# A fused two-block transformer kernel: the front rebuilt around channel-major inputs, and the retention stage reordered

## The reference, cut to what matters

```python
# layer 0 of the first block
mem_n = rmsnorm(mem, g_mem)
h = rmsnorm(x, g_mix[0])
mem_k, mem_v = split(mem_n @ w_mem_kv[0])
p = h @ w_in_a[0]
u, q_mem = p[..., :1536], p[..., 1536:]
a, gate = split(u + b_glu)
v = causal_dwconv(a * sigmoid(gate), w_dw_a, b_dw_a)   # 31 taps, 768 channels
mix = silu(layernorm(v, ln_g, ln_b))
mem_o = memory_attention(q_mem, mem_k, mem_v)          # 4 heads of 64
x = x + concat([mix, mem_o]) @ w_out[0]
x = x + conv_ffn(rmsnorm(x, g_ffn[0]), ...)
# layer 1: forgetting attention, memory attention, conv_ffn, final rmsnorm
# second block, layer 0: retention, 4 heads
s = (q @ k.T) * decay;  o = s @ v                      # in chunks of 128 tokens
o = (o - mu) * rsqrt(var + EPS) * gn_gain
h = h + (silu(gate) * o) @ w_out
# then a per-layer embedding, sparse attention, a second embedding, rmsnorm
```

## Time and profile before

| | |
|---|---|
| median of 3 runs | 1319.33 us (1319.16 to 1319.84) |
| profiled execution, its own time | 1318.41 us |
| its span in the trace | 1316.6 us |
| PE busy in the span | 1246.5 us (95%) |
| DVE, ACT busy | 893.2 us (68%), 641.8 us (49%) |
| granted TensorE clock, mean | 0.977 |
| DMA | 198.44 MB, mean 151 GB/s |

### The profile page before, as it was taken

The page is one execution under the profiler, slowest core; times in us unless marked ns, Lnnn a source line. Parts: engine busy times, 40 slices in busy tenths (PEclk is TensorE's granted clock), DMA queues, the critical chain, the costliest instruction groups (busy, mean ns, idle before and its releaser), DMA issues.

```text
span 1316.6 us, 19422 instructions
## 1 busy us (share of the span) xinstructions
PE 1246.5 (95%) x8046; PEld 1113.3 (85%) x8046; DVE 893.2 (68%) x1361; ACT 641.8 (49%) x999; POOL 11.6 (1%) x27
## 2 busy tenths in 40 slices
PE   4988899999999999999999999979899999999996
PEld 4976798999998768899999977768798989999885
DVE  4996568877765556888778756645576546666664
ACT  5464655555554334455545334324444555555453
POOL 0000000000000000000000000000000000000000
PEclk8988899999989999999999999989999899999999
DMA  8420244555442223365554544524545532222341
GB/s 353 161 96 1 99 160 158 205 207 177 180 160 97 97 96 128 133 219 192 192 187 163 195 160 152 187 74 158 188 161 192 211 149 97 97 97 97 113 178 62
DMA packets 28135, 198.44 MB, mean 151 GB/s; under 512 B 3216, under 2 KB 3344, under 8 KB 4752
## 3 DMA queue, kind: packets, MB, share of 16 engines
q1 hardware_dynamic: 28048, 197.21, 41.6%
HBM read 196.14 MB, written 1.05 MB: 150 GB/s over the span
## 4 chain that ended last, share of the span: by engine, by line
PE 79%; DVE 10%; issue 5%; ACT 4%; DMA 1%; DVEq 0%; SPq 0%; POOL 0%; POOLq 0%; ACTq 0%
PE bank L682 22%; PE bank L683 21%; PE bank L684 21%; DVE WL L1514 3%; ACT WH L1161 3%; PE bank L948 2%; DMA RAW<-wstream 1%; DVE work L1700 1%; PE bank L1135 1%; PE bank L1110 1%; PE bank L886 1%; PE bank L1101 1%; PE bank L1032 1%; PE bank L1118 1%; PE bank L1133 1%
## 5 line engine op out<-in xcount | busy, mean ns | idle before, releaser
L1514 DVE TENSOR_TENSOR WL<-RAW,WH 128x2048 fp32r<-128x2048 f32 x181 | 414.1, 2290 | 204.6 <-ACT WH L1161 204.0
L1161 ACT ACTIVATE WH<-RAW 128x2048 fp32r<-128x2048 f32 x181 | 345.5, 1911 | 221.4 <-PE bank L684 213.3
L682 PE MATMUL bank<-XH,WH 128*128 128x256 f32 x1264 | 361.5, 286 | 12.1 <-DVE XL L1550 7.4
L683 PE MATMUL bank<-XL,WH 128*128 128x256 f32 x1264 | 358.3, 283 | 0.0
L684 PE MATMUL bank<-XH,WL 128*128 128x256 f32 x1264 | 358.1, 283 | 0.0
L682 PEld LDWEIGHTS bank<-XH,WH 128*128 128x128 f32 x1264 | 243.0, 192 | 16.8 <-DVE XL L1550 8.0
L683 PEld LDWEIGHTS bank<-XL,WH 128*128 128x128 f32 x1264 | 243.2, 192 | 0.5
L684 PEld LDWEIGHTS bank<-XH,WL 128*128 128x128 f32 x1264 | 243.1, 192 | 0.0
L682 PE MATMUL bank<-WH,MH 128*128 128x512 f32 (+1 forms) x544 | 203.0, 373 | 9.2 <-DVEq L1633 5.7
L683 PE MATMUL bank<-WL,MH 128*128 128x512 f32 (+1 forms) x544 | 200.0, 368 | 0.0
L684 PE MATMUL bank<-WH,ML 128*128 128x512 f32 (+1 forms) x544 | 199.5, 367 | 0.0
(11 more groups left out here) (254 smaller groups left out, 1559.0 us busy)
## 6 DMA issues: line engine op xcount, KB each, us to landing
RAW<-wstream SPq DMA_DIRECT2D x181, 1024.0 KB, 4.8
con<-consts SPq DMA_DIRECT2D x1, 1681.0 KB, 17.9
x<-x_in SPq DMA_DIRECT2D x1, 1024.0 KB, 4.9
work<-mem_in SPq DMA_DIRECT2D x1, 1024.0 KB, 14.3
out_dram<-xn SPq DMA_DIRECT2D x2, 512.0 KB, 2.7
par<-params SPq DMA_DIRECT2D x1, 868.0 KB, 6.2
gfree<-g_final SPq DMA_DIRECT2D x1, 512.0 KB, 19.0
xn<-p_in SPq DMA_DIRECT2D x2, 256.0 KB, 3.9
```

Source lines behind the costliest of these rows:

```text
L682: mm(o, ah, bh, start=start, stop=False)
L683: mm(o, ah, bl, start=False, stop=False)
L1161: act_fn(WH[:, t % RING, :], RAW[:, t % RING, :], ACT.Copy).then_inc(w_rounded, 1)
L1514: tt(WL[:, t % RING, :], RAW[:, t % RING, :], WH[:, t % RING, :].bitcast(F32), ALU.subtract).then_inc(w_split, 1)
```

## The change

Three things are done together.

1. **Inputs.** The host also gives x and the memory transposed, with channels on the partitions (`xT_in`, `memT_in`, 1 MB each). ACT multiplies xT by the gain into XH and DVE forms XL, with no normalisation before: the factor of each token is spread by two small matmuls (`spread`) and applied when a projection is evicted (`scaled` on DVE, `by_token` on ACT). The transposes of x and the memory, and the scaling to xn, go. The first tile is rounded and split in quarters, and PE's first tile waits by parts. The DMAs are issued in another order: xT, 20 columns of parameters, tiles 0 and 1, x, ident, tile 2, the other parameters, mem, tile 3, memT, then tiles; constants come ahead of tile qm.
2. **Convolution, attention, layer norm.** PE takes 15 taps of block 3 as well (77 matmul taps in place of 62), and they are issued 11 a slot inside the slots of memory attention. DVE keeps 109 taps, 10 of them a slot. The mean's six matmuls wait block by block. The variance is summed over tokens' partitions by 12 matmuls of one column, the power is taken on POOL, spread by matmuls between two halves, and the rest goes by pairs of blocks. Tile mk1 is cut into halves around the variance, and the o0 tiles come in the order 3, 0, 1, 2.
3. **Retention.** The scores rs and the turn of the head before are issued between rv and rg. The last head's turn goes between tiles 5 and 6 of the output projection.

The diff, cut to its core:

```diff
+O0_ORDER = (3, 0, 1, 2)
+PE_CONV = {3: CONV // 2, 4: CONV, 5: CONV}
+TAPS_PER_SLOT = 11
 # SP
-            sp.dma_start(x[:, :, :], ...)
-            sp.dma_start(ident_sb[:, :], ident_in)
-            sp.dma_start(par[:, :], params)
+            sp.dma_start(xT, xT_in).then_inc(xT_loaded, 16)
+            sp.dma_start(par[:, 0:N_FIRST], params[:, 0:N_FIRST]).then_inc(first_par, 16)
+            load(0)
+            load(1)
+            sp.dma_start(x[:, :, :], ...)
+            sp.dma_start(ident_sb[:, :], ident_in)
+            load(2)
+            sp.dma_start(par[:, N_FIRST:], ...)
+            sp.dma_start(memx, ...)
+            load(3)
+            sp.dma_start(memT, memT_in)
+            for t in range(4, NT):
+                if TILES[t] == ("qm", 0):
+                    (con, bfree, gfree)
 # PE
+            def spread(n):
+                o = take(("rb", n))
+                if n == "ln":
+                    pe.wait_ge(ln_rstd_done, 1)
+                else:
+                    rstd_there(pe, n)
+                r = ln_rstd if n == "ln" else rstd[:, n, :]
+                for i in range(TT):
+                    last = mm(o[:, i * P:(i + 1) * P], r[:, i:i + 1].to_broadcast([P, P]), ident, start=True, stop=True)
+                last.then_inc(aux_done, 1)
+            def conv_taps(slot):
+                for n in range(slot * TAPS_PER_SLOT, (slot + 1) * TAPS_PER_SLOT):
+                    b, k = PE_TAPS[n]
+                    if k == 0:
+                        conv_out[b] = take(("cv", b))
+                    last = k == PE_CONV[b] - 1
+                    pe.wait_ge(diag_built, n + 1)
+                    mm(conv_out[b][:, 0:T], diag[:, n % DIAGS, :], vpad[:, b, k:k + T], start=(k == 0), stop=last)\
+                        .then_inc(aux_done if last else diag_used, 1)
 # PE, in a slot of attention, before its scores
+                    if base == 0:
+                        conv_taps(s)
-            norm_full(1)
+            (tile ca0: for each k, wait for XL of k and the tile's quarter)
+            gemm_t_half(("cg", 0), 0, XH, XL)
+            spread(1)
+            gemm_t_half(("cg", 0), 1, XH, XL)
-            norm_full(0)
+            gemm_t_half(("mk", 0), 0, KH, KL, 0)
+            spread(0)
+            gemm_t_half(("mk", 0), 1, KH, KL)
+            for at, b in enumerate((0, 1, 4, 2, 3, 5)):
+                pe.wait_ge(*dve_a.next())
+                last = mm(o[:, 0:T], ones, conv[:, b, :], ...)
+            gemm_t_half(("mk", 1), 0, KH, KL)
+                    last = mm(o[:, i:i + 1], lnsq[:, b, i * P:(i + 1) * P], ones[:, 0:1], ...)
+            gemm_t_half(("mk", 1), 1, KH, KL)
+            spread("ln")
             gemm_v(("mv", 1), KH, KL)
 # ACT
+            for k in range(KD):
+                act_fn(XH[:, k, :], xT[:, k, :], ACT.Copy, scale=col("g_mix0", k))
+            def diags(slot):   # builds the slot's 11, at most 8 ahead of PE
 # ACT, in a slot of attention, before its exponentials
+                    if base == 0:
+                        diags(s)
 # DVE, in a slot of attention, first
+                    if base == 0 and s < n + 3:
+                        taps(TAPS_IN_SLOT)          # 10
+            dve_taps = [(b, i) for i in range(CONV) for b in (0, 1)]
+            dve_taps += [(b, i) for i in range(CONV) for b in (2, 3) if not 0 < i <= PE_CONV.get(b, 0)]
             for j in range(3):
+                scaled(("ca", j), glu_a)
                 upto(("ca", j))
-                taps(8)
+                taps(6)
+                scaled(("cg", j), glu_t)
                 upto(("cg", j))
 ...
+                elif j == 1:
+                    (KL from memT, 8 instructions)
+                taps(6)
+            scaled(("qm", 0), q_mem, DH ** -0.5)
             upto(("qm", 0))
             taps(8)
+            spread(0)
+            scaled(("mk", 0), mkt[:, 0, :, :])
+            upto(("mk", 0))
+            taps(8)
+            upto(("mv", 0))
             (SWL)
-            taps(4 * CONV)
             attention(0, ...)
+            taps(len(dve_taps))
 # retention, PE
                 gemm_n(("rv", h), XH, XL)
-                gemm_n(("rg", h), XH, XL)
                 (rs)
+                if h:
+                    ret_turn(h - 1)
+                gemm_n(("rg", h), XH, XL)
                 (ro)
-                if h:
-                    ret_turn(h - 1)
-            ret_turn(RH - 1)
             o = [take(("ro", q)) for q in range(4)]
-            is_free(pe, ("ry", RH - 1, 1))
+            is_free(pe, ("ry", RH - 2, 1))
             for c in range(7):
+                if c == 6:
+                    ret_turn(RH - 1)
+                    is_free(pe, ("ry", RH - 1, 1))
                 gemm_d(("ro", c), o, MH, ML, 2 * c, c == 0)
```

More of the change, by code:

```diff
@@ L698, in gemm_t_half @@
                 for k in range(KD):
-                    parts(n, k, b == 0)
+                    if n is not None and b == 0:
+                        pe.wait_ge(*front_a.next())
                     s = slice(k * 256 + b * P, k * 256 + b * P + P)
@@ L1321, in _ @@
-            act.drain().then_inc(act_for_pe, 1)
-            attention(0, [("mem", 0, h) for h in range(4)], [NMB, NMB + 1])
-            act.wait_ge(*dve_a.next())
-            act_fn(lnsq, conv, ACT.Square).then_inc(act_for_pe, 1)
-            projected(("mk", 1), mkt[:, 1, :, :])
-            act.wait_ge(*dve_a.next())
-            act_fn(rs_ln, rs_ln, ACT.Sqrt).then_inc(act_for_dve, 1)
-            for pair in range(NMB // 2):
+                if j == 0:
+                    act.wait_ge(mem_loaded, 16)
+                    squares(0, memx)
+                elif j == 1:
+                    act.wait_ge(memT_loaded, 16)
+                    act.wait_ge(par_loaded, 16)
+                    for k in range(KD):
+                        act_fn(KH[:, k, :], memT[:, k, :], ACT.Copy, scale=col("g_mem", k)).then_inc(hi_done, 1)
+                else:
+                    sw = PCOL["w_f"][0]
+                    act_fn(SWH[:, :], par[:, sw:sw + KD * (FOX + 48)], ACT.Copy).then_inc(sw_rounded, 1)
@@ L1337, in _, with ln_high @@
+            def ln_high(p):
+                act_fn(MH[:, pairs[p], :], conv[:, pairs[p], :], ACT.Copy, scale=0.5).then_inc(hi_done, 1)
+            for p in range(2):
                 act.wait_ge(*dve_a.next())
-                c = slice(2 * pair, 2 * pair + 2)
-                act_fn(MH[:, c, :], conv[:, c, :], ACT.Copy, scale=0.5).then_inc(hi_done, 1)
-            projected(("mv", 1), mvv[:, 1, :, :])
-            for c in range(3):
+                ln_tanh(p)
+            act.wait_ge(*dve_a.next())
@@ L1342, in _ @@
+            act.wait_ge(*dve_a.next())
+            ln_high(0)
+            ln_tanh(2)
+            for p in range(1, 3):
+                act.wait_ge(*dve_a.next())
+                ln_high(p)
+            upto(("mv", 1))
+            by_token(("mv", 1), mvv[:, 1, :, :], 0)
+            for c in O0_ORDER[:3]:
                 upto(("o0", c))
-            enter(2, ("o0", 3))
+            enter(2, ("o0", O0_ORDER[3]))
             ffn(0)
@@ L1753, in _ @@
-            link(copy(cmpb[:, :], const("cmpmask")))
-            sync()
+            taps(len(dve_taps))
+            for b in (0, 1):
+                dve.wait_ge(dve_chain, last_of[b])
+                dve.drain().then_inc(dve_for_pe, 1)
+            ready(dve, ("cv", 3))
+            dve.wait_ge(dve_chain, last_of[3])
+            free(tt(conv[:, 3, :], B(("cv", 3))[:, 0:T], conv[:, 3, :], ALU.add), ("cv", 3), "dve")
+            ready(dve, ("cv", 4))
+            free(ts(conv[:, 4, :], B(("cv", 4))[:, 0:T], col("b_dw_a", 4), None, ALU.add), ("cv", 4), "dve")
@@ L1755, in _ @@
+            for n in range(3):
+                dve.drain().then_inc(dve_for_pe, 1)
+            ready(dve, ("cv", 5))
+            free(ts(conv[:, 5, :], B(("cv", 5))[:, 0:T], col("b_dw_a", 5), None, ALU.add), ("cv", 5), "dve")
             dve.drain().then_inc(dve_for_pe, 1)
+            pairs = [slice(2 * p, 2 * p + 2) for p in range(NMB // 2)]
             ready(dve, ("mean",))
-            tt(conv, conv, B(("mean",))[:, 0:T].unsqueeze(1).to_broadcast([P, NMB, T]), ALU.subtract).then_inc(dve_for_act, 1)
+            for c in pairs:
+                tt(conv[:, c, :], conv[:, c, :], B(("mean",))[:, 0:T].unsqueeze(1).to_broadcast([P, 2, T]),
+                   ALU.subtract).then_inc(dve_for_act, 1)
```

394 lines of the change are left out of this document (207 added, 187 removed).

## The result

The changed kernel takes **1309.5 us** (median of 4 runs, 1308.61 to 1309.77), against 1319.3 us before (4 runs, 1319.16 to 1319.84). The ratio is 0.9924, with a 95% interval from 0.9908 to 0.9939. The forecast was 1303.6 with a range from 1295 to 1312: the direction is right and the time lies in the range, but of the 15.7 us that were forecast 9.8 came. The profiled execution took 1308.61 for a span of 1306.7.

A forecast was written before the change was run, and what follows sets the result against it. PE, busy for 95% of the span, was taken as the bound through its work or holes, with DVE pacing the front. The front's 8.5 us and retention's 7.2 summed to 15.7, giving 1303.6 us, range 1295 to 1312.

The forecast's parts named there:

- The start: First transfers and projections: PE's first matmul at 10.3 instead of 21.08, 10.8 us earlier; memory's mean square at about 28.7.
- VectorE's stretch: Front: DVE works 47.1 us without a pause from the memory's mean square to attention unit 0's maximum, ending at 75.8.
- the hole of 4.4: PE's wait before slot 1 of the convolution, from 72.9 to 77.3, with 2.6 us added for a clock fall.
- Then DVE sets the pace: Front, after the start: the start's gain doesn't pass through, since DVE gets projection evictions and keeps nearly all its taps.
- The rival of a smoother hand-over: Convolution slots: DVE reaches unit 0 in time, the 4.4 hole and its low clock go; about 1296 us, chance 0.18.
- The slots: Convolution with memory attention: slots 1 to 3 at 8 us, then 7.2, 6.5 and 5.8; last values done at 123.2.
- Layer norm: From the last values to the exit: mean's end 126.5, variance 2.9, tile split wait 2.7, exit at 164.7.
- The forecast's own 103.7: Convolution: time after slots 1 to 3, from 77.3 at 8 us a slot, with 2.6 for the clock.
- Retention: Retention stage: 5.0 us from the waits ahead of ro and 2.2 at its end, 7.2 us in all.
- the last values near 123: Sign at the end of the convolution slots: PE's last attention values done at 123.2, against 127.3 before.
- the mean's end near 126.5: Sign in layer norm: the mean's last matmuls done 3.3 us after the last values, at 126.5.
- the exit near 165: Sign at the front's end: exit into the next stage at 164.7 against 173.2, a gain of 8.5 us.

The follow-up runs named there:

- the kernel with zeros: Changed kernel with early table load, diagonals ahead of exponentials and tile 12 split early, plus 46 matmuls of zeros on PE during the first transfers: 1295.34 us.
- the kernel with everything: Changed kernel with early table load, diagonals first, tile 12 split early, output projection's banks from the other ring, last head's turn one tile earlier: 1282.58 us.
- a relieved VectorE: Changed kernel with ten convolution taps left out, all those VectorE did in slot 0 (output not the reference's): 1304.24 us in one run.
- The run with the new order: Changed kernel, but ScalarE builds the first 8 diagonals of the next slot ahead of the exponentials of the slot before: 1297.16 us.
- the kernel with retention's ring edit: Changed kernel, but retention's output projection takes its banks from the ring that the last head's turns don't use: 1302.69 us.
- the one with the early table load: Changed kernel with one tiny ACT copy ahead of ACT's first wait, so the activation table loads during the first transfer: 1308.75 us.
- the one with three edits: Changed kernel with early table load, diagonals ahead of the exponentials, and tile 12 split ahead of tanh: 1293.08 us.
- the kernel with retention's order alone: Kernel before the change, with only the changed kernel's retention schedules of PE, ScalarE and VectorE: 1311.75 us.
- with two: Changed kernel with diagonals ahead of the exponentials and tile 12 split ahead of tanh, without the early table load: 1293.80 us.

## Why the forecast held in sign and missed in size

- **The start.** xT's landing and the pace of XH and WL were right. Not seen was that the table load, at 0.73 before, slides behind the transfer that the first activation waits for: 1.28. As a term of the miss it is small: moved back, it gave 0.8, with intervals that overlap. The spread stood at 21.88 and VectorE's mean square of the memory at 30.11 instead of 28.7. Two things end there together: the gate's eviction, behind which ScalarE does its rounding at 24.59, and the fourth tile's transfer, on which the rounding hangs where PE comes early (24.57 in the kernel with zeros, against a forecast landing of 23.0). In the kernel with everything the rounding began at 23.66 and the mean square at 29.18, so the transfer isn't equally late each time. This term was 1.4 too small.
- **VectorE's stretch** was right as a sum: 47.1 forecast, 47.2 measured (30.11 to 77.34). So was its consequence, the hole of 4.4 (3.8), and the low clock behind it.
- **"Then DVE sets the pace" is half of the reason.** The forecast named the coupling, the diagonals of a slot queued behind the exponentials, and put its hole of 2.1 a slot into the sum; for this kernel that held (3.8, 2.1 and 1.5). But it took ScalarE's order as given and blamed VectorE's work. The runs show the order on ScalarE to be what makes the holes: with it changed, a maximum as late leaves 1.5 of the 10.1 us of waits, and without it changed, a relieved VectorE leaves holes of 2.1. The rival of a smoother hand-over, at 1296, has its mechanism in this: it was put down to VectorE being in time, and against it stood that "the 47.1 us hold no wait that could go". The run with the new order gave 1297.2 with VectorE just as late.
- **The slots.** Slots 1 to 3 were forecast at 8 us, the next two at 7.2 and 6.5, and 2.6 once for the clock. Measured from start to start they took 9.89, 9.88, 8.21, 7.22 and 6.39. The low clock came twice, at 1.7 each (6.70 less 5.0), so that it cost 3.4, where the sum had it once, at 2.6; without it the first three slots are 8.2 each. Even the 1.7 of slot 1 varies: behind the same hole of 3.8 its taps took 7.31 us in the kernel with retention's ring edit and 7.75 in the one with the early table load. The slots went on at 78.83 instead of 77.3, and the last values ended at 126.45 instead of 123.2: 1.5 are the later resumption and 1.7 the slots, half of them the second fall of the clock.
- **Layer norm.** From the mean's start on, the terms held: 24 one-column matmuls took 2.73 (2.9 taken, from bounds of 0 and 2.9), the wait for the tile's split 3.16 (2.7). Behind the last values 0.8 was missing for the mean, 1.1 of it a wait for VectorE's evictions. Only the range, and not the sum, held the low clock behind the 3.16, which cost 1.6.
- **The step whose size failed,** then, is the time from VectorE's mean square to the exit. It was forecast as one late start of the slots and one fall of the clock; the start came 1.5 later, the clock fell three times, and the mean took 0.8 more. Together: 1.5 + 1.7 + 0.8 + 0.2 + 1.6 = 5.8, which is the difference of 164.7 and 170.5. The forecast's own 103.7 should read 103.9 (77.3, three slots of 8 and 2.6), and the clock's fall in the earlier trace rows comes 2.0 and not 2.3 us into the hole (0.64 on average from 147 to 149, in a hole that began 5.68 ahead of 151.20); neither changes the picture.
- **Retention** held term by term: waits of 4.0 and 2.2 (3.7 and 2.3 forecast) and one fall of the clock, together 7.2 in the profiles and 7.8 in the medians of the kernel with this alone. That the clock fell once in this profile is luck. Of the nine profiles with these two waits only two, the changed kernel's and the one with three edits, kept it behind the 2.2; in the other seven the stage ends 1.6 us later. The first row is of the changed kernel, the second of the kernel with retention's order alone, both just behind that wait:

```profile
894.00:896.00 2.00, 2.00 (x11) 1.65 (x10) 2.00 (x2) 0.00 (x0) 0.00 (x0) 1.00 0.00 0
...
898.00:900.00 2.00, 2.00 (x6) 1.52 (x6) 2.00 (x2) 0.00 (x0) 0.00 (x0) 0.50 0.00 0
```

- **What would have shown it.** "PE's first matmul at 10 to 11" (11.93), "slots of about 8 us" (9.9 for the first two), "the last values near 123" (126.45), "the mean's end near 126.5" (130.56) and "the exit near 165" (170.52) failed. VectorE's stretch without a pause, the hole, the wait behind the first o0 tile (3.16, a little over its 2 to 3), no wait ahead of ro, and the one ahead of the projection were seen.

## What to carry to other kernels

When an engine does two things in turn, one for a neighbour that is ahead and one that waits for a neighbour that is behind, put the work for the first one ahead by as much as its ring of buffers holds; here that was worth 12.4 us, more than the whole change. When a sum shows that an engine's work ends late, ask next who is queued behind the instruction that waits for it, since that, and not the sum, sets the hole. Price holes like those of 2.1 to 3.8 us here with the chance of a stretch of TensorE at the low clock behind them (1.6 to 2.7 us here), and each bank by when its last reader is done: taking the banks from the other ring gave 6.8 us without an instruction more or less.

## What the runs showed of the hardware

- How long PE is slow at its start varies by a few us. The same matmuls ran 0.214 us apart instead of 0.12, and the last slow one started at 14.4, 14.5, 14.6, 15.2, 15.6, 16.6 and 17.5 us in the seven kernels that begin alike at 11.8 to 11.9. The profile's clock column has 1.00 in these windows, so the slow start is read from the distance of matmuls and not from the column. That such a start varies from run to run is also what the Trainium skill says (TensorE: Matmul & The Clock Gate, What's actually happening); the traces agree.
- Matmuls of zeros brought the clock up before the real ones: the slow ones were gone (12 records in the changed kernel, from 11.93 to 14.41).
- Holes of 3.8 and 2.1 us were followed by taps at the low clock, 6.70 us instead of 5.02 for eleven in the changed kernel. A hole of 1.54 was not in the changed kernel, and was in the kernel with the early table load (taps at 97.82 took 6.70, while those behind its 2.13 took 5.02). Behind the 2.2 us in retention's output projection it fell in seven profiles of ten, not in the changed kernel, the one with three edits and the one with retention's ring edit. So the length of a hole does not decide alone, and what does is open.
- In the kernel with everything, and in the one with matmuls of zeros, the clock fell without a hole. The windows of the former show PE busy through the 24 records of one-column matmuls of the variance (from 120.06), and a window a little behind them has the lower level:

```profile
120.00:122.00 2.00, 2.00 (x21) 2.00 (x20) 0.22 (x1) 1.74 (x1) 0.00 (x0) 1.00 0.00 0
122.00:124.00 2.00, 2.00 (x17) 2.00 (x17) 2.00 (x2) 0.00 (x0) 0.00 (x0) 0.85 0.04 8
124.00:126.00 2.00, 2.00 (x11) 2.00 (x11) 0.14 (x2) 0.00 (x0) 0.69 (x1) 0.50 0.40 78
```

  It cost 1.5 us there. In the kernels with the new order on ScalarE alone, with two and with three edits the same instructions kept the clock. That one-column matmuls bring it down was not tried by itself and stays a guess.
